# Continuing block-product sums in one PSUM bank, with ScalarE copying the partial sums: a change to a fused two-layer transformer kernel on Trainium2

## The reference

```
def swiglu(h, w_gate, w_up, w_down):
    return (jax.nn.silu(h @ w_gate) * (h @ w_up)) @ w_down

for i in range(DEPTH):                      # 2 layers, D_FF = 2816
    ...                                     # token mixer
    x = x + g2 * swiglu(modulate(rmsnorm(x, norm_ffn[i]), sh2, sc2),
                        ffn_w_gate[i], ffn_w_up[i], ffn_w_down[i])
```

## Time and profile before

| | us |
|---|---|
| median of 3 runs (lowest to highest) | 2332.99 (2331.04 to 2333.38) |
| the profiled execution's own time | 2330.7 |
| its span in the trace | 2329.4 |
| PE busy | 2304.8 (99%) |
| DVE busy | 1698.0 (73%) |
| ACT busy | 803.9 (35%) |
| POOL busy | 118.7 (5%) |

### The profile page before, as it was taken

How to read it: one execution, slowest core, us unless ns; L and a number is a source line. 1 busy time by engine, 2 the same in 40 slices (tenths; PEclk the granted TensorE clock), 3 DMA queues, 4 the chain that set the end, 5 groups by cost and what they waited for, 6 DMA issues and landing times.

```text
span 2329.4 us, 29137 instructions
## 1 busy us (share of the span) xinstructions
PE 2304.8 (99%) x10989; PEld 1907.7 (82%) x10989; DVE 1698.0 (73%) x2552; ACT 803.9 (35%) x1293; POOL 118.7 (5%) x90
## 2 busy tenths in 40 slices
PE   8999999999999999999999999999999999999998
PEld 5888888888888888888888788888888888888887
DVE  5777887886598888888886764264897777777777
ACT  6355555552443222222223411111532222222224
POOL 0101101000300000000001200001200000000002
PEclk9999999999999999999999999999999999999999
DMA  7101111132112333333322021121011111111112
GB/s 300 35 27 52 52 43 43 43 129 93 42 37 73 109 109 109 109 109 109 109 91 91 19 73 37 36 73 36 37 51 50 55 46 46 54 49 51 55 37 90
DMA packets 51960, 163.36 MB, mean 70 GB/s; under 512 B 7552, under 2 KB 12032, under 8 KB 51712
## 3 DMA queue, kind: packets, MB, share of 16 engines
q1 hardware_dynamic: 51840, 161.72, 20.7%
HBM read 157.51 MB, written 4.19 MB: 69 GB/s over the span
## 4 chain that ended last, share of the span: by engine, by line
PE 94%; DVE 4%; DMA 1%; ACT 1%; issue 0%; SPq 0%; POOL 0%; DVEq 0%; POOLq 0%; ACTq 0%
PE ps L635 26%; PE ps L637 26%; PE ps L636 26%; PE ps L1132 3%; PE ps L1066 2%; PE ps L1070 1%; PE ps L1068 1%; PE ps L1067 1%; PE ps L1071 1%; PE ps L1111 1%; PE ps L1113 1%; PE ps L1112 1%; DMA ada_ring<-ada_pe 1%; PE ps L902 1%; PE ps L911 0%
## 5 line engine op out<-in xcount | busy, mean ns | idle before, releaser
L2248 DVE SCALAR_TENSOR_TENSOR x<-ps,mods,x 128x512 f32<-128x512 f32 x440 | 322.7, 749 | 146.0 <-PE ps L637 126.7
L635 PE MATMUL ps<-g_hi,w_hi 128*128 128x512 f32 (+1 forms) x848 | 327.5, 386 | 0.1
L637 PE MATMUL ps<-g_hi,w_lo 128*128 128x512 f32 (+1 forms) x848 | 326.5, 385 | 0.0
L636 PE MATMUL ps<-g_lo,w_hi 128*128 128x512 f32 (+1 forms) x848 | 326.5, 385 | 0.0
L635 PE MATMUL ps<-h_hi,op_hi 128*128 128x512 f32 x640 | 249.2, 389 | 0.0
L637 PE MATMUL ps<-h_hi,op_lo 128*128 128x512 f32 x640 | 249.0, 389 | 0.0
L1779 ACT CAST op_hi<-rq 128x512 fp32r<-128x512 f32 x240 | 147.2, 623 | 234.1 <-PE ps L637 228.9
L1790 ACT ACTIVATE g_full<-g_full 128x512 f32<-128x512 f32 x80 | 50.8, 634 | 490.8 <-DVE g_full L2601 490.8
L635 PE MATMUL ps<-h_hi,w_hi 128*128 128x512 f32 x512 | 200.6, 392 | 1.6 <-DVE h_lo L2479 1.5
L637 PE MATMUL ps<-h_hi,w_lo 128*128 128x512 f32 x512 | 199.3, 389 | 0.0
L636 PE MATMUL ps<-h_lo,w_hi 128*128 128x512 f32 x512 | 199.3, 389 | 0.0
(11 more groups left out here) (365 smaller groups left out, 4492.0 us busy)
## 6 DMA issues: line engine op xcount, KB each, us to landing
rq<-stream SPq DMA_DIRECT2D x80, 512.0 KB, 3.6
mod_raw_f<-ada_rows SPq DMA_DIRECT2D x48, 512.0 KB, 3.5
raw<-stream SPq DMA_DIRECT2D x46, 512.0 KB, 3.6
w_lo_f<-stream SPq DMA_DIRECT2D x46, 512.0 KB, 4.4
mod_raw<-ada_rows SPq DMA_DIRECT2D x32, 512.0 KB, 3.5
ada_ring<-ada_pe SPq DMA_DIRECT2D x16, 512.0 KB, 11.3
x<-x_t SPq DMA_DIRECT2D x8, 512.0 KB, 7.3
x0a<-x_t SPq DMA_DIRECT2D x2, 1024.0 KB, 6.2
```

The lines of the kernel that those rows point to most:

```text
L635: nc.tensor.matmul(out, w[0][wi], a[0][ai], start=start, stop=False)
L636: nc.tensor.matmul(out, w[0][wi], a[1][ai], start=False, stop=False)
L637: return nc.tensor.matmul(out, w[1][wi], a[0][ai], start=False, stop=stop)
L2248: nc.vector.scalar_tensor_tensor(out=x[:, m, HALF[half]], in0=ps[:, out_bank(d, m), :], scalar=mods[:, gate + m:gate + m + 1], in1=x[:, m, ...
```

## The change

S2, S3 and A22 are no longer started as sums of their own: they are added by PE onto A11 in the same bank (bank 0 for gate, 1 for up), and S4 onto S1 (bank 2 or 3). So PSUM holds U2 after S2, U3 after S3 and C21 after A22. ACT copies the state after S2 to `part_u` and after S3 to `part_w` (`part_keep`, semaphore `kept`), and PE waits for the copy before it goes on in that bank. DVE adds only C11, C22 and C12; C21 is read straight out of PSUM by ACT's silu and DVE's product. Gate and up alternate product by product (S2 gate, S2 up, S3 gate, S3 up). As up S2 is now product 5 of a block and not 6, its `sums` stand ahead of `operand_low(s, 5)`. The core of the diff:

```diff
-PRODUCTS = ((GATE, "A11"), (GATE, "A12"), (UP, "A11"), (UP, "A12"), (GATE, "S2"), (GATE, "S3"), (UP, "S2"),
-            (UP, "S3"), (GATE, "S1"), (UP, "S1"), (GATE, "A22"), (UP, "A22"), (GATE, "S4"), (UP, "S4"))
+PRODUCTS = tuple((mat, name) for mat in (GATE, UP) for name in ("A11", "A12"))\
+    + tuple((mat, name) for name in ("S2", "S3", "S1", "A22", "S4") for mat in (GATE, UP))
+CHAIN = ("A11", "S2", "S3", "A22")
+def product_bank(mat, name):
+    return mat if name in CHAIN else 2 + mat
...
 def one_product(s, mat, name, job=None):
...
+            out, more = ps[:, product_bank(mat, name), :], name not in ("A11", "A12", "S1")
...
 def bank_read(s, mat, name):
...
+            if name == "S2":
+                pe.wait_ge(part_1, 2 * s + mat + 1)
+            elif name in ("S3", "A22"):
+                pe.wait_ge(kept, kept_n(s, mat, "S2" if name == "S3" else "S3"))
+            elif name in ("S1", "S4"):
+                pe.wait_ge(part_in, read_n(s, "C11" if name == "S1" else "C22", mat))
...
+        def part_keep(s, mat, name):
+            act.wait_ge(prod, product_n(s, mat, name) + 1)
+            if name == "S2":
+                act.wait_ge(part_in, read_n(s, "C11", mat))
+            copy(part_u[mat][:] if name == "S2" else part_w(s, mat), ps[:, product_bank(mat, name), :]).then_inc(kept, 1)
...
 # ACT, wino_block
-            for n in range(8, 12):
-                operand_top(s, n)
+            for n, (name, mat) in enumerate((("S2", GATE), ("S2", UP), ("S3", GATE), ("S3", UP))):
+                part_keep(s, mat, name)
+                operand_top(s, n + 8)
...
 # DVE, wino_block, blocks that are not the first
-                for n in range(2, 6):
+                for n in range(2, 5):
                     operand_low(s, n)
+                sums(s, UP)
+                operand_low(s, 5)
...
 # DVE, wino_block, the first block of a feed-forward
                 operand_low(s, 4)
+                sums(s, UP)
                 operand_low(s, 5)
                 dve.wait_ge(dn, 8 * d_was + KD)
                 part(s, "C11", GATE)
-                sums(s, UP)
                 part(s, "C11", UP)
                 operand_low(s, 6)
                 corner_mult(s, "C11")
-                part(s, "U2", GATE)
                 operand_low(s, 7)
```

More of the change, by code:

```diff
@@ L277 @@
 N_PROD = len(PRODUCTS)
[L278 to L283, removed]
+READS = tuple((corner, mat) for corner in ("C11", "C22", "C12") for mat in (GATE, UP))
+READ_OF = {"C11": "A12", "C22": "S1", "C12": "S4"}
+KEPT = ("S2", "S3")
+CHAIN = ("A11", "S2", "S3", "A22")
 CORNERS = ("C11", "C22", "C21", "C12")
@@ L304, in product_n, with kept_n @@
     return N_PROD * s + products_of(s).index((mat, name))
[L307 to L313, removed]
+def product_bank(mat, name):
+    return mat if name in CHAIN else 2 + mat
 def read_n(s, what, mat):
-    return len(READS) * s + (READS_END if at_end(s) else READS).index((what, mat)) + 1
+    return len(READS) * s + READS.index((what, mat)) + 1
+def kept_n(s, mat, name):
+    return 4 * s + 2 * KEPT.index(name) + mat + 1
 def corner_at(s, corner):
@@ L631, in bias_of, with mm3 @@
         return bias_sb[:, tile, of:of + 1]
[L633 to L637, removed]
+    def mm3(out, w, wi, a, ai, start, stop, more=False):
+        nc.tensor.matmul(out, w[0][wi], a[0][ai], start=start and not more, stop=False, skip_group_check=more)
+        nc.tensor.matmul(out, w[0][wi], a[1][ai], start=False, stop=False, skip_group_check=more)
+        return nc.tensor.matmul(out, w[1][wi], a[0][ai], start=False, stop=stop, skip_group_check=more)
     def tile_of(dram, n):
@@ L1414, in wino_block @@
             down_of(d_was, A)
[L1415 removed]
+            products(s, (UP, "A11"), (UP, "A12"), (GATE, "S2"), (UP, "S2"))
             if at_end(s):
@@ L1788, in corner_gate @@
             gate = g_full[GATE][:, CORNER_F[corner], HALF[CORNER_HALF[corner]]]
-            act.wait_ge(part_in, read_n(s, corner, GATE))
-            nc.scalar.activation(gate, gate, ACT.Silu).then_inc(corner_act, 1)
+            if corner == "C21":
+                act.wait_ge(prod, product_n(s, GATE, "A22") + 1)
+                if not at_end(s):
+                    act.wait_ge(part_in, read_n(s, "C22", GATE))
+                src = ps[:, product_bank(GATE, "A22"), :]
+            else:
+                act.wait_ge(part_in, read_n(s, corner, GATE))
+                src = gate
+            nc.scalar.activation(gate, src, ACT.Silu).then_inc(corner_act, 1)
         def corner_split(s, corner):
@@ L2606, in corner_mult @@
             gate, up = (g_full[mat][:, f, cols] for mat in (GATE, UP))
-            dve.wait_ge(part_in, read_n(s, corner, UP))
             dve.wait_ge(corner_act, corner_n(s, corner))
-            nc.vector.tensor_tensor(up, up, gate, ALU.mult).then_inc(corner_full, 1)
+            if corner == "C21":
+                dve.wait_ge(prod, product_n(s, UP, "A22") + 1)
+                if not at_end(s):
+                    dve.wait_ge(part_in, read_n(s, "C22", UP))
+                src = ps[:, product_bank(UP, "A22"), :]
+            else:
+                dve.wait_ge(part_in, read_n(s, corner, UP))
+                src = up
+            nc.vector.tensor_tensor(up, src, gate, ALU.mult).then_inc(corner_full, 1)
         def corner_low(s, corner):
@@ L2705, in wino_block @@
             corner_low(s, "C22")
-            part(s, "C21", GATE)
             operand_low(s + 1, 0)
-            part(s, "C21", UP)
             corner_mult(s, "C21")
```

68 lines of the change are left out of this document (20 added, 48 removed).

## The result

| | before | changed |
|---|---|---|
| median of 20 runs each (lowest to highest) | 2331.99 us (2330.61 to 2337.73) | 2337.98 us (2335.81 to 2340.19) |
| profiled execution: own time / span | 2330.7 / 2329.4 | 2338.7 / 2337.4 |

The ratio is 1.0025, with a 95% interval of 1.0019 to 1.0031: the kernel became 6.0 us slower. 2339.2 was predicted.

A forecast was written before the change was run, and what follows sets the result against it. PE was taken to bound the kernel. First blocks +2.3, loaded turns +2.7, second-layer scales +0.4 and light turns +0.8 sum to +6.2 us on 2333.0, giving 2339.2 us; the range was 2333.5 to 2344.

The forecast's parts named there:

- first blocks: First block of each feed-forward (s = 0 and 10): 1.69 us lost where 0.53 was before, +2.3 us for two.
- late `part_uu` copy / S2 copy / T1: PE's waits in each first block: up S2 on up A11's copy 1.24, S3 gate 0.40, S1 gate 0.05 us.
- loaded turns: Turns between blocks where DVE's list has no gaps: tile 4 waits for `to_x`, 0.34 us each, +2.7, last another +0.4.
- light turns: Turns between blocks where DVE waits for PE anyway: tile 4 waits 0.08 us for `to_x`, +0.8 us in 10.
- copies in ordinary blocks: ACT's copy after S2 gate, while S2 up runs: takes 0.97 of 2.72 us, so costs nothing if ACT is free.
- Pace of the matmuls: In the 20 blocks: matmuls stay 0.2267 us apart whatever DVE does, so taking work off DVE won't make PE faster.
- signs of being wrong: Wrong if a turn's first `to_x` starts before 10.0 us, matmuls aren't 0.2267 apart, or an ordinary-block copy leaves under 0.3 us.
- only the first blocks pay: Rival, chance 0.30: DVE is 0.35 us earlier at the turns, which cost nothing; +2.3 us left, 2335.3 us.
- copies are late everywhere: Rival, chance 0.07: ACT is held over 1.75 us before copies at 40 S3 products; 2351 to 2378 us.
- the matmuls get faster with less on DVE: Rival, chance 0.02: DVE's lighter load raises matmul pace by one part in 250 over the 20 blocks, to 2328.
- the 39 us: Cost if 40 S3 products each lost 0.97 us to uncovered copies, as the banks rule taken strictly would have it.
- the missing sum ahead of T1 makes the first blocks free: Rival, chance 0.10: no late copy in first blocks, S1 gate on time, turns free; -1.1 us for two, 2331.9 us.

The follow-up runs named there:

- experiment 3: Changed kernel with up's sums behind the first four `to_x` at turns, and ACT's copies and DVE's list reordered in first blocks: 2331.27 us, ratio 0.9996 to the kernel before.
- experiment 2: Changed kernel, but in first blocks ACT makes T1's top and the `part_uu` copy ahead of up's S2 operand: 2335.32 us, ratio 1.0017 to the kernel before.
- experiment 1: Changed kernel, but in the 18 turns up's sums and the split behind them follow the first four `to_x`: 2335.24 us, ratio 1.0013 to the kernel before.
- experiment 4: Changed kernel with operand 3's low part made twice on DVE, with a wait between, in each of 18 turns: 2351.38 us, ratio 1.0084 to the kernel before.
- experiment 6: Changed kernel with ACT making gate's S2 copy five times in a row in all 20 blocks: 2357.61 us, ratio 1.0109 to the kernel before.
- experiment 5: Kernel before with only the new product order and up's sums ahead of the fifth operand split, no chain or copies: 2344.97 us, ratio 1.0055 to the kernel before.

## Why the prediction was right, and which terms were off

| term (us, against before) | predicted | measured |
|---|---|---|
| first blocks, each | +1.16 | +1.17, +1.16 |
| of which late `part_uu` copy / S2 copy / T1, less the 0.53 of before | 1.24 / 0.40 / 0.05 | 1.12 / 0.42 / 0.06, and 0.10 in longer steps |
| loaded turns, 8 together, with the scale vectors | +3.1 | +2.2 |
| light turns, 10 together | +0.8 | +0.2 |
| copies in ordinary blocks | 0 | 0 |
| clock | not in the sum | about +1 in the medians (estimate) |
| sum | +6.2 | +4.7 by waits, +6.0 in the medians |

**Pace of the matmuls, DVE's relief.** As predicted: 105 us less on DVE gave nothing by themselves (experiment 3). Of ACT's 47 us of copies the page's busy time shows 32; where copies and casts follow each other they overlap (the copy of 696.20 lasts 0.58, and ACT's next row stands at 696.67). I didn't trace the rest of that difference.

**First blocks.** Right in place, order and size; experiment 2 takes the `part_uu` part away and leaves the S2 copy, experiment 3 takes both. That the total agrees to 0.01 us is luck: the copy's term was 0.12 too large, and the longer steps behind the stalls, 0.10, had no term. The T1 term, written as 0.05, comes to 0.02 by the figures given for it, and 0.06 was measured.

**Turns.** Right in mechanism (experiments 1 and 4), too large in size. The step that was mis-sized is the way from up's S2 sum to the split. I took 0.10 us for the release of DVE by ACT, and had the split at 857.83 and `to_x` at 858.43, which is 4.81 us after the half projection. The rows show the top from 858.55 to 859.17 and the split at 859.21: 0.04 us. So `to_x` comes at 4.72, 0.09 us earlier, of which 0.06 is this release and 0.03 the sums ahead of it. The cost of a `to_x` that ends at 5.47 for a tile due at 5.44 is 0.21, which by the rule means a constant of 0.18 rather than the 0.22 that I had from T1. In the light turns both together put the first `to_x` just inside its room, where 0.08 was reckoned. The last loaded turn, with the scale vectors, lost 0.6 (0.74 predicted). One of the prediction's own signs of being wrong came true by this: a first `to_x` that starts before 10.0 us after the block's start. In the loaded turns it starts at 10.16, in the light ones at 9.92 (4.48 + 5.44). The sign was set too close, since the prediction's own figure for the light turns, 1882.45 for a block that starts at 1872.46, is 9.99.

**The clock.** The sum had no term for it. Over the runs with a clock on record its mean is 0.9981 for the kernel before (53 runs, all from the experiments) and 0.9976 for the changed one (20 runs); 0.0005 of 2335 us is an estimate of 1.1 us. Among runs whose clock is 0.998, the medians are 2332.2 (28 runs) and 2337.48 (13), 5.3 us apart, nearer to the 4.7 of the waits. So the predicted +6.2 stands near the measured +6.0 in part by luck: 1.5 us too much for waits met 1.3 us that had no term. Most of the 1.2 us between 2339.2 and 2337.98 is the starting point, a median of three runs that lay 1.0 over that of twenty. Why the changed kernel has a little less clock isn't settled (more waits of PE would be one reason, and no run tests it), and some tenths stay open.

**The rivals.** That only the first blocks pay is out: experiments 1 and 2 give back 2.7 us each by the medians (2.4 and 2.0 by the same matmuls) when one half is undone. That copies are late everywhere is out: experiment 3 has no such wait at any of the 80 copies, and experiment 6 shows 1.7 us of room at the 16 copies where it was used up. That the matmuls get faster with less on DVE is out by the constant distance in experiment 3. (The Trainium skill, Perfetto Trace Analysis, section "Matmuls", advises rotating PSUM banks between independent groups, so that the copy out of one overlaps the matmuls of the next. The trace agrees with that purpose: gate's copy of 0.59 us runs beside up's product in another bank. What it does not bear out is the 39 us that the prediction got by reading the advice as a rule against going on in one bank: 12 matmuls of the other matrix between are enough.) That the missing sum ahead of T1 makes the first blocks free became true only with the orders of experiment 3.

## What to carry to other kernels

A change that takes work off an engine that isn't the last can still cost time, by the order that it forces: price each instruction that moves past one that the bound engine waits for, release by release, on every queue. Continuing a sum in a PSUM bank after its copy costs nothing as long as copy, handoffs and whatever stands ahead of the copy in its queue fit into the work between (here 1.0 of 2.7 us). Where a loss is a list that ends a few tenths too late, look at how much slack the other places have too: experiment 4 shows ten turns that lost next to nothing and had less than 0.1 us left.

## What the runs showed of the hardware

**A wait of PE can be followed by a stretch at half clock.** In experiment 6 the first blocks make PE wait for 2.6 us, and both times TensorE then runs at half of its clock, 1.2 GHz, for about 3.4 us. PE, first block of that kernel, and the windows (busy us of PE, PEld, DVE, ACT, POOL; granted clock; DMA):

```profile
700.86 0.79 PE L634 MATMUL ps<-h_hi,op_hi 128*128 128x512 f32 x1 [2.59 <-ACT part_ug L1820]
701.45 0.63 PE L635 MATMUL ps<-w_lo,op_hi 128*128 128x512 f32 x1
...
703.92 0.39 PE L635 MATMUL ps<-w_lo,op_hi 128*128 128x512 f32 x1
```

```profile
699.00:702.00 3.00, 1.14 (x3) 0.95 (x4) 2.67 (x6) 2.94 (x6) 0.00 (x0) 0.73 0.00 0
702.00:705.00 3.00, 3.00 (x11) 2.41 (x10) 2.85 (x3) 0.33 (x1) 0.00 (x0) 0.70 0.00 0
```

The windows' clocks, 0.73 and 0.70, are means over full speed and half speed; 0.27 and 0.30 of 3 us, doubled, are 3.4 us at half speed. By the same sum the clock fell at about 700.4, while PE still waited. The matmuls behind the wait stand 0.43 us apart instead of 0.23 until 703.6, and the stall costs 1.4 to 1.6 us beyond the wait. This wait cost more than its length.

**After one and the same shorter wait the stretch is there in some profiled executions and not in others.** At the start of the convolution stage PE waits 1.11 us for `h_lo` in both kernels. In the profiled execution of the kernel before no slow stretch follows it; in that of the changed kernel one does. The windows of before, then PE and the windows of the changed kernel:

```profile
1300.00:1305.00 5.00, 5.00 (x24) 4.14 (x23) 5.00 (x6) 1.46 (x3) 4.36 (x3) 1.00 0.00 0
```

```profile
1300.98 0.50 PE L633 MATMUL ps<-h_hi,w_hi 128*128 128x512 f32 x1 [1.11 <-DVE h_lo L2494]
...
1301.80 0.63 PE L633 MATMUL ps<-h_hi,w_hi 128*128 128x512 f32 x1
1302.22 0.63 PE L634 MATMUL ps<-h_lo,w_hi 128*128 128x512 f32 x1
```

```profile
1300.00:1305.00 5.00, 4.01 (x11) 3.19 (x12) 5.00 (x4) 2.29 (x4) 4.51 (x4) 0.68 0.00 0
1303.00:1305.00 2.00, 2.00 (x6) 1.53 (x5) 2.00 (x3) 0.64 (x1) 1.67 (x2) 0.50 0.00 0
```

It costs 1.65 us there. Experiments 3 and 4 show the same stretch at this place, experiments 1, 2, 5 and 6 and both executions of the kernel before don't. Experiment 3 has no wait in its blocks, so the stretch doesn't need those waits.

The second step marked clock lies at the end of the program. Windows of the changed kernel, and of the same work in the kernel before:

```profile
2321.00:2326.00 5.00, 4.79 (x28) 4.50 (x28) 4.04 (x8) 1.61 (x5) 1.14 (x2) 0.66 0.52 199
```

```profile
2314.00:2319.00 5.00, 4.36 (x37) 4.16 (x38) 4.52 (x9) 1.40 (x5) 1.62 (x2) 1.00 0.52 197
```

A stretch like this stands there in the changed kernel and in experiments 1, 2, 4, 5 and 6, and in neither execution of the kernel before nor in experiment 3. Each changed program was profiled once, so whether the change brings this stretch about stays open. One such event is more than a quarter of the whole effect under study, and a single profiled execution can't be compared with another without looking for it first.
